# RWKV-7 time mix on one core: the first group's diagonal blocks are gathered by ScalarE and masked by VectorE in one copy

## What is computed

```python
def step(S, inp):
    r_t, d_t, k_t, v_t, kk_t, a_t = inp
    Sk = jnp.einsum('bhij,bhj->bhi', S, kk_t)
    S = S * d_t[:, :, None, :] - Sk[..., None] * (kk_t * a_t)[:, :, None, :] + v_t[..., None] * k_t[:, :, None, :]
    return S, jnp.einsum('bhij,bhj->bhi', S, r_t)
```

## Time and profile before

| | |
|---|---|
| time, median of 3 runs | 1483.86 us (1481.19 to 1487.07) |
| time of the profiled execution | 1483.12 us, of which its span is 1481.5 us |
| TensorE busy | 1448.7 us, 98% of the span, 14518 matmuls |
| VectorE busy | 858.0 us, 58%, 1730 instructions |
| ScalarE busy | 555.9 us, 38%, 1356 instructions |
| GpSimd busy | 370.8 us, 25%, 482 instructions |
| granted TensorE clock, mean | 0.992 of full |
| the eight rounds of the time mix | from about 657 to 1225 us |

### The profile page before, as it was taken

The page is one execution under the profiler, slowest core; times in us unless marked ns, Lnnn a source line. Parts: engine busy times, 40 slices in busy tenths (PEclk is TensorE's granted clock), DMA queues, the critical chain, the costliest instruction groups (busy, mean ns, idle before and its releaser), DMA issues.

```text
span 1481.5 us, 36383 instructions
## 1 busy us (share of the span) xinstructions
PE 1448.7 (98%) x14518; PEld 1078.5 (73%) x14518; DVE 858.0 (58%) x1730; ACT 555.9 (38%) x1356; POOL 370.8 (25%) x482
## 2 busy tenths in 40 slices
PE   7999999999999999999999999999999999999998
PEld 4555577777888888777777777777777777777753
DVE  3154566668777777474858676767676522023533
ACT  3166555541222222256363535454545232210000
POOL 0000141220111111125132221213131046355452
PEclk9999999999999999999999999999999999999999
DMA  9813698833466664421121212111112225342311
GB/s 328 319 57 110 169 263 286 248 99 111 125 161 163 157 157 128 118 56 39 36 55 32 54 33 53 42 44 42 45 40 59 55 83 171 86 153 75 121 43 50
DMA packets 191519, 165.35 MB, mean 112 GB/s; under 512 B 38550, under 2 KB 169622, under 8 KB 190327
## 3 DMA queue, kind: packets, MB, share of 16 engines
q1 hardware_dynamic: 182343, 128.15, 30.9%
q0 software_dynamic: 8352, 32.52, 7.4%
q10 hardware_dynamic: 656, 2.36, 0.5%
HBM read 136.91 MB, written 26.08 MB: 110 GB/s over the span
## 4 chain that ended last, share of the span: by engine, by line
PE 88%; DVE 7%; DVEq 1%; ACT 1%; issue 1%; DMA 0%; SPq 0%; POOL 0%; ACTq 0%
PE me_bank L3275 13%; PE rw_bank L1915 11%; PE sa_psOs L1250 8%; PE sa_psS L1203 7%; PE pr_psZ L754 4%; PE me_bank L3313 3%; PE fr_bankL L317 3%; PE fr_bankL L251 2%; DVE rw_gram L2777 2%; PE rw_bank L1951 2%; PE pr_psS L742 2%; PE sa_psT L1213 2%; PE rw_bank L1927 2%; PE rw_bank L2010 1%; PE rw_bank L2029 1%; PE pr_psO L777 1%
## 5 line engine op out<-in xcount | busy, mean ns | idle before, releaser
L1915 PE MATMUL rw_bank<-hT,big 128*128 128x288 f32 x336 | 97.7, 436 | 0.0
L1311 ACT COPY kpe<-sa_psS 128x512 f32<-128x512 f32 x64 | 34.4, 589 | 134.0 <-PE sa_psS L1203 134.0
L1915 PEld LDWEIGHTS rw_bank<-hT,big 128*128 128x128 f32 x336 | 63.3, 199 | 17.7 <-ACT big L2424 1.7
L1040 POOL DMA_DIRECT2D big<-in_cache_kv x68 | 37.6, 553 | 145.8 <-issue 145.8
L754 PE MATMUL pr_psZ<-hT,qlT 128*128 128x288 f32 x256 | 73.9, 408 | 0.0
L3351 ACT COPY big<-me_bank 128x288 f32<-128x288 f32 x42 | 16.7, 398 | 144.8 <-PE me_bank L3275 144.8
L1040 POOL DMA_DIRECT2D pages<-in_cache_kv x68 | 37.5, 552 | 117.1 <-issue 117.1
L754 PEld LDWEIGHTS pr_psZ<-hT,qlT 128*128 128x128 f32 x256 | 46.6, 189 | 20.2 <-issue 8.5
L1250 PE MATMUL sa_psOs<-big,sa_ST 128*128 128x257 f32 x256 | 60.3, 385 | 0.0
L1250 PE MATMUL sa_psOs<-pages,sa_ST 128*128 128x257 f32 x256 | 60.3, 385 | 0.0
L1407 DVE TENSOR_TENSOR sa_ST<-sa_psT,kinvp 128x512 f32<-128x512 f32 x64 | 42.9, 679 | 23.6 <-PE sa_psT L1213 23.6
(11 more groups left out here) (653 smaller groups left out, 3702.7 us busy)
## 6 DMA issues: line engine op xcount, KB each, us to landing
big<-in_w_in SPq DMA_DIRECT2D x44, 512.0 KB, 3.9
big<-in_cache_kv POOLq DMA_DIRECT2D x68, 128.0 KB, 4.6
pages<-in_cache_kv POOLq DMA_DIRECT2D x68, 128.0 KB, 3.4
fr_wada<-in_w_ada SPq DMA_DIRECT2D x8, 1024.0 KB, 11.4
big<-in_cache_kv SPq DMA_DIRECT2D x60, 128.0 KB, 3.0
pages<-in_cache_kv SPq DMA_DIRECT2D x60, 128.0 KB, 3.1
qk_scratch<-oaT SPq DMA_DIRECT2D x32, 192.0 KB, 2.6
fr_wada<-in_w_ada SPq DMA_DIRECT2D x2, 2048.0 KB, 13.2
```

Of the source, the lines that this page charges most:

```text
L1040: e.dma_start(M.pages[s % 2][q * QP:(q + 1) * QP, g, :, 0:KL], src).then_inc(landed, 16)
L1311: nc.scalar.copy(S.rearrange("q (c p j) -> q p c j", c=2 * GP, p=GP)[:, :, cs, :], got[:, :, cs, :]).then_inc(copied, 1)
L1915: last = mm(into, held, moving, start=(k == 0 and n in (1, 2, 7)), stop=(k == K4 - 1), skip_group_check=True)
```

## The change

ScalarE gets a new step at the head of each round, `gather_diagonals(i)`: it waits for the first four grams, copies the diagonal blocks of the first group from `gram` into the tile `W` (four copies of 32x128, one for each quarter of the partitions), where they stand in equal columns on all partitions, and raises `x_reset`. `begin_inverse(i, 0)` waits for that and masks all four quarters of `W` into `X` in one copy of 128x128. The other two groups are begun as before. In rounds 1 to 7 the call on VectorE moves behind the copies of grams 6 and 7, in a call of their own with its drain; in round 0 the order stays. `x_reset` now counts two in each round.

```diff
--- before.py
+++ after.py
@@ -2456,6 +2456,12 @@
                         act.wait_ge(uvm_sb, i)
                     a.copy(uv[halves[1], :], b[halves[1], 3 * P:4 * P]).then_inc(tm_sb, 1)
 
+            def gather_diagonals(i):
+                act.wait_ge(gram_sb, NU * i + GR[0].stop)
+                for r in quads:
+                    last = a.copy(W[r, GR[0], :], gram[r, GR[0], 2, r])
+                last.then_inc(x_reset, 1)
+
             def level(i, lv):
                 for gr in groups_of(lv):
                     n = GR[gr].stop - GR[gr].start
@@ -2587,6 +2593,7 @@
             a.activation(osq[:, 0, 0:1], M.vec[:, 0:1], ACT.Sigmoid)
             for i in range(NP):
                 p, more = i + 1, i < LAST
+                gather_diagonals(i)
                 for c in range(C5):
                     if i == 0 and c == 3:
                         bonus_sums(0)
@@ -2782,9 +2789,12 @@
 
             def begin_inverse(i, gr):
                 us, n = GR[gr], GR[gr].stop - GR[gr].start
-                dve.wait_ge(x_reset, i + 1)
-                for r in quads_of(gr):
-                    v.copy_predicated(X[r, us, :], bc(lev[r, 0, :], n, 1), gram[r, us, 2, r])
+                dve.wait_ge(x_reset, 2 * i + (1 if gr else 2))
+                if gr == 0:
+                    v.copy_predicated(X[:, us, :], bc(lev[:, 0, :], n, 1), W[:, us, :])
+                else:
+                    for r in quads_of(gr):
+                        v.copy_predicated(X[r, us, :], bc(lev[r, 0, :], n, 1), gram[r, us, 2, r])
                 dr()
                 transposed(gr).then_inc(x_sb[gr], 1)
 
@@ -2943,8 +2953,9 @@
                     add_value_partial(i, 22)
                     mix_last_values(i)
                     grams(i, range(4, 6))
+                    grams(i, range(6, 8))
                     begin_inverse(i, 0)
-                    grams(i, range(6, NU))
+                    grams(i, range(8, NU))
                     begin_inverse(i, 1)
                 else:
                     grams(0, range(0, 6))
```

## The result

| | before | changed |
|---|---|---|
| median | 1483.8 us (4 runs, 1481.2 to 1487.1) | 1475.6 us (4 runs, 1474.3 to 1476.6) |
| ratio | | 0.9949, 95% interval 0.9930 to 0.9969 |
| profiled execution, span | 1481.5 us | 1472.7 us |
| mean granted TensorE clock, profiled execution | 0.992 | 0.999 |
| TensorE / VectorE / ScalarE busy | 1448.7 / 858.0 / 555.9 us | 1440.0 / 852.1 / 564.6 us |

8.2 us faster, where 2.65 was forecast: the right direction, and outside the range (1477.0 to 1486.0).

The account below looks back on a forecast made before the run. TensorE was taken as busy 98% of the span, with the chain on VectorE some 13 us each time-mix round. Savings 2.1 + 0.65 - 0.1 = 2.65 us gave 1480.5 profiled, 1481.2 us as median; range 1477.0 to 1486.0.

Parts of the forecast that it names:

- The chain: Time mix, eight rounds: VectorE's earlier finish reaches TensorE; 2.1 + 0.65 - 0.1 = 2.65 us saved.
- forecast 0.35: Rounds 2 to 7: gram 8, waiting for TensorE's fifth gram block, starts 0.35 us earlier; six rounds give 2.1 us.
- forecast 0.65: Round 1: TensorE is relatively ahead, so gram 8 starts earlier by 0.64 to 0.72 us, taken as 0.65.
- forecast 0.1 lost: Round 0: the gather delays ScalarE's sigmoids and TensorE's second lora_part; 0.1 us lost, bounds 0.3 gained and 0.4 lost.
- Copies: begin_inverse(i, 0): one masked 128x128 VectorE copy of 0.30 us replaces four taking 1.23 us, saving 0.93 a round.
- gather: Four ScalarE copies take 1.22 us behind the gate's sigmoid in rounds 1 to 7, within 3.37 us idle; VectorE never waits.
- gate: Rounds 2 to 7: gram 8 must await TensorE's fifth gram block, capping VectorE's some 0.7 us gain at 0.35.
- hand-over: Time from a TensorE matmul's end to the waiting engine's start, ahead of gram 8: 0.04 to 0.14 us.
- lower figure for a VectorE copy: Trainium skill's estimate of 0.19 us per 128-column copy, so three fewer save 0.58 us; the forecast used the rows instead.
- the sum: Round savings of 2.65 us reach the end whole, through dense TensorE work behind: 1480.5 profiled, 1481.2 as median.
- No rival: Three rivals: all VectorE's saving arrives, 1479.1 us, chance 0.15; nothing arrives, 1484.1, 0.22; late gather, 1491.6, 0.04.
- The slow rival: A late gather holds up begin_inverse and VectorE behind it; at 1.2 us a copy 1483.9 + 7.7 = 1491.6; chance 0.04.

Follow-up runs that it names:

- before, again: The kernel before, unchanged, measured and profiled once more: 1483.1 us, ratio 1.0012.
- gather only: Changed kernel with begin_inverse(i, 0) left ahead of grams 6 and 7, ScalarE's gather and the single masked copy kept: 1474.1 us, ratio 0.9949.
- not in round 0: Changed kernel without the gather in round 0, which keeps its four VectorE copies: 1475.0 us, ratio 0.9951.
- changed, filled: Changed kernel plus one unread 128x160 matmul where TensorE waits for the second group in rounds 1 to 7: 1474.5 us, ratio 0.9952.
- before, filled: Kernel before plus one unread 128x288 matmul where TensorE waits for the second group in rounds 1 to 7: 1478.3 us, ratio 0.9980.
- changed, delayed: Changed kernel plus a repeated 32x128 VectorE copy and drain ahead of begin_inverse(i, 1) in rounds 1 to 7, two in round 1: 1484.2 us.
- move only: Kernel before with begin_inverse(i, 0), still four VectorE copies, moved behind grams 6 and 7 in rounds 1 to 7; no gather: 1489.3 us.
- before, delayed: Kernel before plus one repeated 32x128 VectorE copy and drain ahead of begin_inverse(i, 1) in rounds 1 to 7: 1493.7 us, ratio 1.0063.
- block 5 early: Changed kernel with TensorE's fifth gram block ahead of multiply(i, VZ, 4) in rounds 1 to 7: 1474.6 us, ratio 0.9942.
- gather in place, block 5 early: Changed kernel with begin_inverse(i, 0) ahead of grams 6 and 7, and the fifth gram block ahead of multiply(i, VZ, 4) in rounds 1 to 7: 1471.8 us.

## Why the prediction was wrong, step by step

| kernel | median, us | mean clock | longest wait at the first levels, rounds 1 to 7 | rounds 1 to 7 with a fall (profile) | mean time at equal clock |
|---|---|---|---|---|---|
| before (71 runs beside the experiments) | 1482.3 | 0.9933 | 0.76 to 0.98 | 3 of 7 | 1473.9 |
| before, again | 1483.1 | 0.9925 | 0.74 to 0.98 | 3 of 7 | 1474.1 |
| changed | 1475.6 | 0.9970 | 0.41 | 0 of 7 | 1471.8 |
| gather only | 1474.1 | 0.9978 | 0.41 | 0 of 7 | 1471.3 |
| not in round 0 | 1475.0 | 0.9972 | 0.41 | 0 of 7 | 1471.7 |
| changed, filled | 1474.5 | 0.9975 | filled | 0 of 7 | 1471.5 |
| before, filled (11 runs) | 1478.3 | 0.9969 | filled (0.30 left in round 1) | 0 of 7 | 1475.2 |
| changed, delayed | 1484.2 | 0.9926 | 0.78 to 1.15 | 2 of 7 | 1474.6 |
| move only | 1489.3 | 0.9886 | 0.96 to 1.32 | 4 of 7 | 1475.4 |
| before, delayed | 1493.7 | 0.9860 | 1.13 to 1.35 | 6 of 7 | 1474.3 |
| block 5 early | 1474.6 | 0.9977 | 0.20, in round 5 0.57 | 1 of 7, behind "issue" | 1471.2 |
| gather in place, block 5 early | 1471.8 | 0.9972 | 0.20 | 2 of 7, behind "issue" | 1468.2 |

The last column takes the clock out: over the runs of each kernel by themselves, a mean clock lower by 0.001 goes with 1.26 us more (1.31 over the 71 runs of the kernel before), and the mean time is brought to clock 1 by that slope. 0.001 of 1480 us is 1.48 us of full-speed work lost, so most of it is paid. It is a fit and an estimate, good to about 1 us (the changed kernel has only four runs, and the filled kernel before stands 1.4 us above the kernel before, for which I have no cause); the order of the column bears out the chain's part, and it makes plain that from 1474 to 1494 us nearly everything is clock.

**The chain (forecast 2.65 us).** Held. From the fifth gram block to the third group's first level the changed kernel gained 0.38 us in round 2 (forecast 0.35) and 4.33 - 3.63 = 0.70 in round 1 (forecast 0.65); rounds 3 to 7 gained 0.35, 0.35, 0.32, 0.37 and 0.37. Round 0 lost 0.05 from the block to the second `lora_part` (663.97 to 670.28 before, 665.68 to 672.04 now; forecast 0.1 lost), and there TensorE does wait for ScalarE's sigmoids:

```profile
672.04 0.76 PE L1879 MATMUL rw_bank<-big,rw_wlo 64*128 64x288 f32 x4 [0.56 <-ACT prep L2361]
```

That makes 2.8 us, and the column at equal clock says 1473.9 - 1471.8 = 2.1.

**Copies, gather, gate.** One copy 0.30 us (forecast 0.30); gather 1.20 (1.22), no wait for it on VectorE; TensorE's hand-over 0.05 us (0.04 to 0.14 allowed); gram 8 gated by the fifth block, as said, and as the trace of the run with block 5 early bears out. The prediction's lower figure for a VectorE copy (0.19 us, from 58 cycles in the Trainium skill, VectorE: DVE Perf Modes, the section on the TRN2 errata) did not hold: the new copy took 0.30. The same section says that this entry comes out too short and that about 150 cycles were measured, which makes an estimate of 0.29 us for 128 columns; with that the trace agrees.

**The step that failed: the sum.** "Behind these stretches the chain is dense TensorE work ..., all hung on what has just been shifted" took the dense work's length for given. It was not: its clock depends on the wait ahead of it, and the change shortened just that wait. The missing term is (0.9970 - 0.9933) x 1000 x 1.26 = 4.7 us, larger than the one that I worked out; 2.1 to 2.8 and 4.7 make 6.8 to 7.5, where 6.7 was measured against the 71 runs and 8.2 against the first four. No rival named it. The chain's share came out round by round as worked out, which is no luck; the direction is owed to it, and the size of the whole gain is not. The slow rival's sum, too, had no term for the clock; its 7.7 us would probably have brought more falls with it, as the delay did in the kernel before (2.6 us of delay, 11.4 of time).

**Where it could have been read.** The page's row of 40 slices shows the clock at 9 tenths or more throughout, and I stopped there:

```profile
PEclk9999999999999999999999999999999999999999
```

The windows of 5 us show 0.50, and the timeline of round 2, on which the whole forecast rests, has the two rows of `lora_part` at 0.76 and 1.33 us in it, 1.7 us apart. And the spread of the kernel before, 1481 to 1487 us, which I took for the noise of measuring, is largely its clock: by the slope above, its runs' 0.988 to 0.997 are 11 us.

The Trainium skill (TensorE: Matmul & The Clock Gate, in its section on HAM oscillation) describes a loop in which TensorE waits in each turn, loses half of its clock and starts the next work slowly. The traces here agree in kind: in the profiles of the two slowest kernels, with waits of 0.96 us and more, 10 of 14 rounds have a fall, against none of 35 where the wait is 0.41 us or filled. (The 14 rounds with block 5 early, with waits of 0.20 us and one of 0.57, have three, all behind the pauses named "issue".) The waits ahead of the falls here were 0.74 to 1.35 us, among 32x32 matmuls, and falls followed in some rounds and not in others; why one round and not its neighbour, with waits alike to 0.02 us, is not settled by these runs. Each kernel was profiled once, so these counts are of single executions; what stands on many runs is the mean clock.

## What to carry to other kernels

Ahead of any sum on a chain that hands over between TensorE and a slower engine, ask the granted clock in windows of a few microseconds behind each wait, not in slices of 37, and compare the lengths of like matmuls in it; in the profile of the kernel before a fall cost some two to four times the length of the wait ahead of it (1.4 to 3.0 us behind waits of 0.78 to 0.98). If the waits can't be shortened, fill them: one matmul a round that no one reads, in a bank that is free, won 3 to 4 us here. And where the medians of one unchanged kernel spread by 0.4%, set times beside clocks before calling it noise.

## What the runs showed of the hardware that was not expected

- TensorE's clock falls to 0.50 of full for some microseconds behind a stretch of small matmuls with waits of 0.74 us and more, in 3 of 7 rounds at 0.74 to 0.98 us (in each of two profiles), 2 of 7 at 0.78 to 1.15, 4 of 7 at 0.96 to 1.32, 6 of 7 at 1.13 to 1.35, and in none of 35 at 0.41 us (21) or with the wait filled (14). The 18 falls counted here lengthened the stretch from the second `lora_part` to the next `level_x`, 3.6 to 3.9 us without one and without pauses, by 0.7 to 1.6 us (seven of them) or by 2.9 to 3.1 (eleven).
- It falls at other places too: around 700 to 705 us, in round 0, in five of the profiles (of the gather alone and of the move alone among them), behind 0.6 us of waiting for ScalarE (in the profile of the gather alone); around 605 to 610 us, ahead of the time mix and of everything that the change touches, in four (the kernel before once more, both delayed kernels, the move alone); and in round 0 in two of the six profiles in which TensorE waits 1.0 us for the second group there. So the mean clock counts more than the falls at the first levels. No experiment was made on these.
- A mean clock lower by 0.001 went with 1.26 us of time in this kernel of 1480 us.
- TensorE pauses of 0.3 to 1.1 us for which no engine is named ("issue") occur within the 32x32 matmuls in some rounds.
